# The order of TensorE's work within an attention step: extra product second, values third, transposes last

## The reference

```python
def _attend(q, k, v):
    s = jnp.einsum('bqkgd,bskd->bkgqs', q, k).astype(jnp.float32) * ATTN_SCALE
    p = jax.nn.softmax(s, axis=-1).astype(v.dtype)
    return jnp.einsum('bkgqs,bskd->bqkgd', p, v)

y = attention(h) @ w_o
sh1, sc1, g1, sh2, sc2, g2 = split(silu(c) @ w_mod + b_mod)
x = x + g1 * y
x = x + g2 * experts(modulate(x, norm_ffn, sh2, sc2))
```

## Time and profile before

| | us |
|---|---|
| median of 3 runs | 1870.11 (1867.53 to 1871.41) |
| the profiled execution | 1869.12 |
| its span | 1867.4 |
| attention loop of ab, scores to output projection | 69.6 to 90.7 |
| the same of nsa | 406.9 to 486.7 |
| the same of gqa | 803.5 to 878.6 |
| TensorE busy | 1508.5 (81%) |
| VectorE busy | 459.3 (25%) |
| ScalarE busy | 243.7 (13%) |
| DMA | 711.03 MB, 381 GB/s on the mean |

### The profile page before, as it was taken

How to read it: one execution, slowest core, us unless ns; L and a number is a source line. 1 busy time by engine, 2 the same in 40 slices (tenths; PEclk the granted TensorE clock), 3 DMA queues, 4 the chain that set the end, 5 groups by cost and what they waited for, 6 DMA issues and landing times.

```text
span 1867.4 us, 22822 instructions
## 1 busy us (share of the span) xinstructions
PE 1508.5 (81%) x9954; PEld 716.4 (38%) x9954; DVE 459.3 (25%) x980; ACT 243.7 (13%) x524; POOL 83.6 (4%) x136
## 2 busy tenths in 40 slices
PE   8998777999999778989978677786799667667685
PEld 5654434764454434445522213221264222122221
DVE  2441011467421113874400000000043000000001
ACT  0410000126222011154100000000011000000000
POOL 1100000202000000111100000000000000000000
PEclk9999899999999899999998878887899878778787
DMA  7589999999579999597799999999988999999997
GB/s 294 211 308 426 426 427 424 373 355 372 211 287 419 426 426 421 181 410 288 270 429 431 431 430 430 431 431 430 420 349 335 430 430 431 430 431 430 432 426 291
DMA packets 114541, 711.03 MB, mean 381 GB/s; under 512 B 8240, under 2 KB 13344, under 8 KB 73472
## 3 DMA queue, kind: packets, MB, share of 16 engines
q1 hardware_dynamic: 108208, 697.14, 90.3%
q0 software_dynamic: 4128, 9.73, 1.5%
q10 hardware_dynamic: 2096, 2.57, 0.4%
HBM read 708.17 MB, written 1.05 MB: 380 GB/s over the span
## 4 chain that ended last, share of the span: by engine, by line
PE 45%; DMA 45%; DVE 5%; issue 2%; ACT 2%; SPq 1%; POOL 0%; DVEq 0%; ACTq 0%; PEldq 0%; POOLq 0%
DMA ring<-in_moe_w 23%; DMA work<-in_moe_w 9%; PE pb L809 8%; DMA ring<-in_moe_w_down 7%; PE pa L841 6%; DMA work<-in_moe_w_down 3%; PE acc L1512 3%; PE pb L788 2%; PE acc L1506 2%; PE acc L927 2%; PE pa L863 2%; PE acc L1410 2%; PE acc L1399 1%; PE acc L1227 1%; DMA mod<-in_moe_w_up 1%
## 5 line engine op out<-in xcount | busy, mean ns | idle before, releaser
L809 PE MATMUL pb<-ring,XT 128*32 128x256 f32 (+1 forms) x2528 | 340.1, 520 | 85.7 <-DMA ring<-in_moe_w 78.6
L841 PE MATMUL pa<-ring,work 128*32 128x512 f32 x928 | 197.2, 713 | 62.6 <-DMA ring<-in_moe_w 40.0
L809 PEld LDWEIGHTS pb<-ring,XT 128*32 128x32 f32 x2528 | 104.5, 116 | 286.9 <-issue 135.9
L809 PE MATMUL pb<-work,XT 128*32 128x512 f32 (+1 forms) x544 | 140.5, 613 | 20.9 <-DMA work<-in_moe_w 20.5
L974 DVE TENSOR_TENSOR work<-work,pb 128x256 f32<-128x256 f32 (+1 forms) x32 | 17.8, 555 | 548.9 <-PE pb L809 442.6
L927 PE MATMUL acc<-XT,work 128*128 128x512 f32 x256 | 118.4, 605 | 32.3 <-DVE XT L990 19.4
L863 PE MATMUL pa<-work,HM 128*128 128x128 f32 x896 | 113.0, 288 | 16.3 <-issue 16.3
L863 PEld LDWEIGHTS pa<-work,HM 128*128 128x128 f32 x896 | 112.1, 204 | 31.1 <-issue 31.1
L841 PE MATMUL pa<-work 128*32 128x512 f32 x320 | 94.7, 735 | 25.5 <-DMA work<-in_moe_w 16.7
L936 ACT COPY XT<-pa 128x512 f32<-128x512 f32 x32 | 18.8, 586 | 703.0 <-PE pa L863 694.4
L841 PEld LDWEIGHTS pa<-ring,work 128*32 128x32 f32 x928 | 43.1, 127 | 167.5 <-issue 75.1
(11 more groups left out here) (426 smaller groups left out, 1759.8 us busy)
## 6 DMA issues: line engine op xcount, KB each, us to landing
ring<-in_moe_w SPq DMA_DIRECT2D x135, 2048.0 KB
work<-in_moe_w SPq DMA_DIRECT2D x46, 2048.0 KB
ring<-in_moe_w_up SPq DMA_DIRECT2D x28, 2048.0 KB
ring<-in_moe_w_gate SPq DMA_DIRECT2D x26, 2048.0 KB
ring<-in_moe_w_down SPq DMA_DIRECT2D x24, 2048.0 KB
ring<-in_w_mod SPq DMA_DIRECT2D x40, 1024.0 KB
mod<-in_moe_w SPq DMA_DIRECT2D x11, 2048.0 KB
work<-in_moe_w_down SPq DMA_DIRECT2D x8, 2048.0 KB
```

Source lines behind the costliest of these rows:

```text
L809: last = nc.tensor.matmul(hbank[m][j * CAP:(j + 1) * CAP, :], m_xg[:, k, j * CAP:(j + 1) * CAP], slot_of(per * m + j // held)[:, at:at + f ...
L841: last = nc.tensor.matmul(pa[j * CAP:(j + 1) * CAP, h, :], m_ht[:, c, j * CAP:(j + 1) * CAP], slot_of(i)[:, at:at + 512], start=(c == 0), ...
```

## The change

In `att_tensor` the three groups behind the scores change places. Before: transposes of i - 2, values of i - 3, `extra`. Now: `extra`, values of i - 3, transposes of i - 2. All waits stay with their groups. The programs of the other engines are untouched.

```diff
--- before.py
+++ after.py
@@ -1390,6 +1390,17 @@
                     for dst, lhs, rhs, *first in sp["scores"](i, s_banks(i)):
                         last = nc.tensor.matmul(dst, lhs, rhs, start=first != [False], stop=True, skip_group_check=bool(first))
                     last.then_inc(s_done, 1)
+                if sp["extra"]:
+                    sp["extra"](pe, i)
+                j = i - 3
+                if j >= 0:
+                    pe.wait_ge(s_ptc, n0 + j + 1)
+                    done = j // sp["per_pair"]
+                    if j % sp["per_pair"] == 0 and done:
+                        pe.wait_ge(s_out, ph.out0 + ph.nout - n // sp["per_pair"] + done)
+                    for dst, lhs, rhs, first, end in sp["values"](j, sp["pt"][:, j % 2, :]):
+                        last = nc.tensor.matmul(dst, lhs, rhs, start=first, stop=end, skip_group_check=True)
+                    last.then_inc(s_pv, 1)
                 j = i - 2
                 if 0 <= j < n:
                     pe.wait_ge(s_norm, n0 + j + 1)
@@ -1400,17 +1411,6 @@
                     if sp["more_blocks"]:
                         last = sp["more_blocks"](pe, j, last)
                     last.then_inc(s_pt, 1)
-                j = i - 3
-                if j >= 0:
-                    pe.wait_ge(s_ptc, n0 + j + 1)
-                    done = j // sp["per_pair"]
-                    if j % sp["per_pair"] == 0 and done:
-                        pe.wait_ge(s_out, ph.out0 + ph.nout - n // sp["per_pair"] + done)
-                    for dst, lhs, rhs, first, end in sp["values"](j, sp["pt"][:, j % 2, :]):
-                        last = nc.tensor.matmul(dst, lhs, rhs, start=first, stop=end, skip_group_check=True)
-                    last.then_inc(s_pv, 1)
-                if sp["extra"]:
-                    sp["extra"](pe, i)
 
         def att_scalar(act, ph, sp):
             n0, n = ph.att0, ph.natt
```

## The result

The changed kernel takes 1934.2 us (median of 6, 1929.3 to 1939.7) against 1869.5 before (median of 6): a ratio of 1.035 (95% interval 1.033 to 1.037), 65 us slower. The profiled execution has a span of 1931.8 us, 64.4 more than before.

The account below looks back on a forecast made before the run. The prediction took TensorE to bound the attention steps, with no DMA slack behind them. To 1869.1 us it added 53 for the three loops, 3 for the clock and 1 for the median: 1926 us, range 1907 to 1945.

Parts of the forecast that it names:

- The ring: Block steps: transposes, exponentials, weights' copy, heads' copy, block copy, block product, values wait in a circle; 7.12 us against 4.95 (gqa).
- The block steps: Steps with a block product: 7.12 us for 4.95 in grouped-query (gqa), 7.2 for 4.80 in sparse (nsa).
- The handovers: Block steps of gqa: weights' copy to next ScalarE instruction 0.90 us, heads' copy 0.27, block copy to block product 0.70.
- The bare steps: Steps 11 to 14 of gqa, no block product: 4.8 us for 3.66; four such steps in nsa about +0.8 each.
- The whole loops: Attention stages longer by 5 us (ab, the first), 25 (nsa, sparse) and 23.5 (gqa, grouped-query), taken as 53 in sum.
- The 5 of ab: First attention stage: output products of steps 4 and 5 wait for heads' copies, two waits of 2.2 us, rounded to +5.
- The clock: TensorE's clock during the new idle times: 3 us added, about two products at 1.2 instead of 2.4 GHz.
- The clock rival: TensorE's clock falls in the ring, one in three of 17 block steps slow: 24 us more, 1947 us; chance 0.12.
- The rule of the Trainium skill: On TensorE, small idle times between matmul groups, repeated often, can make the clock swing between its levels.
- Taken back behind the attention: Rival: next stage's loads set when experts begin, hiding up to half of the 53 us: about 1897 us; chance 0.08.
- It does nothing: Rival: the groups are bound by TensorE's unchanged sum alone: 1870 us; chance 0.04.
- It is faster: Rival: the extra product covers the weights' copy, so 7.7 us of TensorE idle time go: 1862 us; chance 0.04.

Follow-up runs that it names:

- Experiments 3: Changed kernel with ScalarE's block copy moved from the end of its step to the beginning, ahead of the exponentials; TensorE's order left as changed: 1892.9 us.
- experiment 4: Changed kernel with ScalarE's step in the order block copy, heads' copy, weights' copy, exponentials; TensorE's order left as changed: 1863.4 us.
- Experiments 7: Changed kernel with ScalarE's block copy split into 8 pieces of 64 columns: 1946.8 us.
- 8: Kernel before the change, with ScalarE's block copy split into 8 pieces of 64 columns: 1870.0 us, ratio 1.000.
- experiment 5: Changed kernel with the scores of gqa and nsa steps computed again from step 2 on, as added TensorE work during its waits: 1924.6 us.
- 6: Kernel before the change, with only ScalarE's weights' copy moved ahead of its exponentials: 1860.0 us.

## Why the prediction was right

*Direction and mechanism.* Forecast 1926 (1907 to 1945), measured 1934.2. The ring was there as described: exponentials released by the transposes, block product released by L1238, scores straight behind the transposes. Experiments 3 and 4 open it in the block steps by ScalarE's program order alone, with TensorE's order as changed; the kernel before has ScalarE's order and no ring. So it takes both. Experiments 7 and 8 show that the block copy is a member of it in the changed kernel and not in the one before.

*The block steps.* Predicted 7.12 in gqa and 7.2 in nsa; measured 7.1 and 7.2 at the full clock. The handovers, which I had as estimates (0.90 from weights' copy to the next instruction, 0.27 for the heads' copy, 0.70 from block copy to block product), are 0.90, 0.26 and 0.67 (896.04, 896.94, 897.20, 897.87).

*The bare steps.* 4.8 predicted in gqa and measured. (4.80 less 3.66 is +1.14, where my sum had +1.05: 0.4 us over four steps. Measured, the four intervals take 19.2 us for 14.8, +4.4.) In nsa I took +0.8 by estimate; the transposes of 476.60, 481.91 and 486.51 are 5.31 and 4.60 apart, 5.0 on the mean, for 3.9 before, about +1.0.

*The whole loops.* Predicted +5, +25 and +23.5, measured +5.2, +32.8 and +26.8. With the clock's share out (the 9.1 and 1.8 that experiment 5 took away), some 24 and 25 are left, 54 with ab. So the sum of 53 was right to about 1 us, in part because small errors go against each other (nsa 1 below my term, gqa 1.5 above). The 5 of ab was a round figure, and its parts were not as I had them: three waits of 2.83, 1.16 and 1.25 us for two of 2.2.

*The clock* is the term that was mis-sized: I added 3 us, "about two products at the lower clock", and it was about 10. The reading on which I leaned, that 3.38 us busy of 5 at 460 to 465 kept 1.00, was one place in the kernel before. In nsa's loop after, 32 of 113 us ran at 1.2 GHz. I had also put the idle pieces at 2.1 us or less; in nsa's block steps they are 2.2 to 2.5. Yet their length alone does not tell when the clock falls: from 448 to 472 three pieces of 2.40 to 2.46 passed and it stayed at 1.00, to fall behind the fourth, and the slowest stretch, 486 to 499 at 0.61, stands in the bare steps, behind pieces of 1.91 and 2.06. The clock rival had the right direction at about 40% of its price. The rule of the Trainium skill ("TensorE: Matmul & The Clock Gate", section "A second HAM failure mode: psum-queue depth-cycling"), which I had set beside that row, is the one that the trace after agrees with in the main: in nsa the granted clock goes down and up again four times after the start (0.79 over 440 to 448, 1.00 over 448 to 472, 0.76 over 472 to 479, 1.00 over 479 to 486, 0.61 over 486 to 499, 0.72 over 512 to 518). Experiment 5 takes these back by filling the pieces.

*The rivals.* "Taken back behind the attention" is out: the loops grew by 64.8 and the span by 64.4. "It does nothing" is out. "It is faster" needed the copies ahead of the exponentials; experiment 4 makes just that and gives 1863, where I had 1862 for that case.

## What to carry to other kernels

When groups of work change places on one engine, write down what each of its waits has queued behind it on the *other* engine, in that engine's program order, and follow it round: a wait that ends last only because of an instruction that stands ahead of its releaser for no reason is mended there, as experiments 4 and 6 do. Of two versions that differ in order alone, one number for each kind of step decided here: the length of the longest ring, against the longest engine's own sum. And a pipelined step that starts to idle by 2 us in 7 can pay again through TensorE's clock, here 10 us on 55.

## What the runs showed of the hardware

With idle pieces of TensorE of 2.2 to 2.5 us in each block step of nsa (7.2 us at the full clock) and of 1.2 to 2.1 in its bare steps, the granted clock was 0.86 over 113 us. In gqa, with pieces of 1.9 to 2.2 and 1.4 to 1.8 us, it was 0.95 over 102 us. The same pieces did not always bring it down: three of 2.40 to 2.46 us in a row passed at 1.00 (448 to 472), and it fell behind the fourth. With the pieces of the block steps filled to 1.1 to 1.4 us it was 0.98 in both. Work that nobody needed, 750 matmul records for 550 in nsa, made the program 9.6 us faster than the changed kernel. A 512-column copy of ScalarE in eight pieces of 64 columns took 1.03 us against 0.59 in one.
